# Pooling stage of a three-block network: window means as products of high and low parts, weight products by chunks, one root in place of an iteration

## The reference, cut to what matters

```
def rmsnorm(x, g):
    y = xf * lax.rsqrt(jnp.mean(xf * xf, axis=-1, keepdims=True) + NORM_EPS)
    return y * g

def pool_mixer(h, w_group, scale):          # h: the normed input, 4 groups of 256 channels
    csum = jnp.cumsum(hf, axis=1)
    for g, w in enumerate((2, 4, 8, 16)):   # mean over the last w tokens
        means.append((cg - prev) / cnt)
    mixed = pooled - hf
    y = jnp.einsum('blgc,gcd->blgd', mixed, w_group)
    return y * scale
...
h = h + rmsnorm(m, norm_mix_post[i])
```

## Time and profile before

| | us |
|---|---|
| median of 3 runs | 961.72 (961.63 to 963.1) |
| profiled execution | 959.84 |
| its span | 958.1 |
| products with `window_means` (L808) | 377.06 to 386.80 |

### The profile page before, as it was taken

The page is one execution under the profiler, slowest core; times in us unless marked ns, Lnnn a source line. Parts: engine busy times, 40 slices in busy tenths (PEclk is TensorE's granted clock), DMA queues, the critical chain, the costliest instruction groups (busy, mean ns, idle before and its releaser), DMA issues.

```text
span 958.1 us, 20030 instructions
## 1 busy us (share of the span) xinstructions
PE 920.1 (96%) x7354; PEld 890.3 (93%) x7354; DVE 685.8 (72%) x1168; ACT 513.3 (54%) x851; POOL 305.7 (32%) x215
## 2 busy tenths in 40 slices
PE   6999999999999998999999999999989999999996
PEld 6987798999999997899999999989989999999995
DVE  7766527999995225699999523879787878885666
ACT  5765555666665426666666544553355445454433
POOL 4117752000004543300001464331236333445643
PEclk9999999999999999999999999999999999999998
DMA  7541032444454541054455454344135455565431
GB/s 261 174 148 44 1 133 96 174 173 174 174 207 181 182 168 45 28 193 175 175 179 205 181 199 159 105 177 148 61 139 177 176 181 197 191 221 186 164 132 45
DMA packets 22147, 146.80 MB, mean 153 GB/s; under 512 B 2752, under 2 KB 5328, under 8 KB 6736
## 3 DMA queue, kind: packets, MB, share of 16 engines
q1 hardware_dynamic: 22096, 146.11, 42.9%
HBM read 143.94 MB, written 1.05 MB: 151 GB/s over the span
## 4 chain that ended last, share of the span: by engine, by line
PE 81%; DVE 12%; ACT 3%; issue 2%; POOL 1%; DMA 0%; POOLq 0%; SPq 0%; DVEq 0%; ACTq 0%
PE bank L439 22%; PE bank L440 22%; PE bank L441 22%; PE bank L693 2%; PE bank L679 2%; DVE u_low L1324 2%; DVE w_low L1315 2%; DVE h L1397 1%; PE bank L527 1%; ACT w_high L952 1%; DVE bank L1389 1%; DVE conv_out L1446 1%; PE bank L808 1%; PE bank L541 1%; PE bank L709 1%
## 5 line engine op out<-in xcount | busy, mean ns | idle before, releaser
L439 PE MATMUL bank<-u_high,w_high 128*128 128x256 f32 (+2 forms) x1400 | 401.1, 286 | 11.7 <-DVE u_low L1324 8.9
L440 PE MATMUL bank<-u_low,w_high 128*128 128x256 f32 (+2 forms) x1400 | 398.9, 285 | 0.0
L441 PE MATMUL bank<-u_high,w_low 128*128 128x256 f32 (+2 forms) x1400 | 397.6, 284 | 0.0
L1823 POOL TENSOR_TENSOR w_low<-raw,w_high 128x512 fp32r<-128x512 f32 (+1 forms) x73 | 199.8, 2738 | 543.7 <-ACT w_high L952 543.7
L1315 DVE TENSOR_TENSOR w_low<-raw,w_high 128x1024 fp32r<-128x1024 f32 (+5 forms) x119 | 189.9, 1596 | 125.5 <-ACT w_high L952 124.3
L439 PEld LDWEIGHTS bank<-u_high,w_high 128*128 128x128 f32 x1400 | 265.5, 190 | 14.3 <-DVE u_low L1324 8.4
L440 PEld LDWEIGHTS bank<-u_low,w_high 128*128 128x128 f32 x1400 | 265.1, 189 | 0.0
L441 PEld LDWEIGHTS bank<-u_high,w_low 128*128 128x128 f32 x1400 | 264.9, 189 | 0.0
L952 ACT ACTIVATE w_high<-raw 128x1024 fp32r<-128x1024 f32 (+5 forms) x119 | 195.2, 1640 | 72.0 <-PE bank L441 61.0
L439 PE MATMUL bank<-x_high,w_high 128*128 128x256 f32 (+1 forms) x608 | 173.9, 286 | 5.1 <-ACT x_high L1252 2.5
L441 PE MATMUL bank<-x_high,w_low 128*128 128x256 f32 (+1 forms) x608 | 173.2, 285 | 0.0
(11 more groups left out here) (213 smaller groups left out, 1057.7 us busy)
## 6 DMA issues: line engine op xcount, KB each, us to landing
raw<-w_up_dram SPq DMA_DIRECT2D x66, 1024.0 KB, 4.8
raw<-w_down_dram SPq DMA_DIRECT2D x24, 1408.0 KB, 6.0
raw<-w_gin_c_dram SPq DMA_DIRECT2D x4, 1536.0 KB, 6.5
raw<-w_wo_dram SPq DMA_DIRECT2D x4, 1024.0 KB, 5.1
raw<-w_wout_dram SPq DMA_DIRECT2D x4, 1024.0 KB, 4.9
raw<-w_pgate_dram SPq DMA_DIRECT2D x4, 1024.0 KB, 4.8
raw<-w_gin_v_dram SPq DMA_DIRECT2D x2, 1024.0 KB, 4.8
raw<-w_gin_g_dram SPq DMA_DIRECT2D x2, 1024.0 KB, 4.8
```

The source lines that it names most:

```text
L439: nc.tensor.matmul(out, hi, rhi, start=start, stop=False)
L440: nc.tensor.matmul(out, hi, rlo, start=False, stop=False)
L441: return nc.tensor.matmul(out, lo, rhi, start=False, stop=stop)
L1823: nc.gpsimd.tensor_tensor(wl[n % 2][:, at], raw[n % 2][:, at], wh[n % 2][:, at].bitcast(F32), ALU.subtract).then_inc(low_parts_g, pool_cou ...
```

## The change

1. **Means.** `pool_z` becomes two tiles, high (ScalarE) and low (VectorE, six new instructions of 512 columns). The means get a high part (three activations in `down0`) and a low part of the first 16 columns, the only ones whose values need one. Each chunk takes seven fp32r products in place of three fp32 ones, over the columns that a window reaches: 144, 144, 16, then 144, 144, then 16, 16. Chunks wait for the low parts.
2. **Weights' products by chunks.** Chunks 0 to 3 multiply for all three token tiles as they come, chunks 4 to 7 for the first tile; the sums follow, then the other two tiles of the second half.
3. **Root.** `a1` is normed by a square root on ScalarE and a reciprocal on VectorE in place of the iteration. VectorE makes the first half of `up1`'s low part ahead of that, the second half after the pooling.
4. **Results.** ScalarE only squares, into five buffers in place of two; VectorE writes the eight scaled copies.
5. The load of the means moves from behind the loads of `down0` to behind those of `up0`.

```diff
-BY_SQRT = ("c", "post0", "fpost0", "post1", "fpost1", "out")
+BY_SQRT = ("c", "post0", "fpost0", "a1", "post1", "fpost1", "out")
...
+REACH = [(0, P + 16), (P, P + 16), (2 * P, T1 - 2 * P)]
...
-                if name == "down0":
+                if name == "up0":
 
                     sp.wait_ge(*done("att out 7 low"))
                     sp.dma_start(wm[:, :, :], dram["window_means"]).then_inc(tables_in, 16)
...
+            for c in range(DC // 2):
+                pool_chunk(c, (0, 1, 2))
+            for c in range(DC // 2, DC):
+                pool_chunk(c, (0,))
+            norm_sums("a1", f"a1 acc {DC - 2}", squares(0, T1), True)
+            for t in (1, 2):
+                for c in range(DC // 2, DC):
+                    pool_chunk(c, (t,))
             pe.wait_ge(tables_in, 80)
+            pe.wait_ge(*done("window means low"))
             for c in range(DC):
                 half, g = c // 4, c // 2
 
-                pe.wait_ge(freed["a"], BLOCKS[first + half * len(TT) + len(TT) - 1]["freed"])
+                pe.wait_ge(*done(f"pool low {max(c, 2) if half == 0 else 5}"))
                 b = first + 2 * len(TT) + c
                 bank_free(b)
-                for t, (t0, nt_) in enumerate(TT):
-                    last = nc.tensor.matmul(bank[BLOCKS[b]["bank"]][:, t0:T1], pz[0:nt_, t, c * P:(c + 1) * P],
-                                            wm[0:nt_, g, WIN_AT[t]:WIN_AT[t] + T1 - t0],
-                                            start=t == 0, stop=t == len(TT) - 1)
+                out, cs = bank[BLOCKS[b]["bank"]], slice(c * P, (c + 1) * P)
+                for t, (t0, w) in enumerate(REACH):
+                    nt_ = TT[t][1]
+                    means = wmh[0:nt_, g, REACH_AT[t]:REACH_AT[t] + w]
+                    nc.tensor.matmul(out[:, t0:t0 + w], pzh[0:nt_, t, cs], means, start=t == 0, stop=False,
+                                     skip_group_check=True)
+                    last = nc.tensor.matmul(out[:, t0:t0 + w], pzl[0:nt_, t, cs], means, start=False,
+                                            stop=t == len(TT) - 1, skip_group_check=True)
+                    if t == 0:
+
+                        nc.tensor.matmul(out[:, 0:16], pzh[:, 0, cs], wml[:, g, :], start=False, stop=False,
+                                         skip_group_check=True)
                 last.then_inc(products, 1)
...
+                if l == 0:
+                    act.wait_ge(tables_in, 80)
+                    for t, (_, w) in enumerate(REACH):
+                        nc.scalar.activation(wmh[:, :, REACH_AT[t]:REACH_AT[t] + w], wm[:, :, WIN_AT[t]:WIN_AT[t] + w],
+                                             ACT.Copy).then_inc(*S.step("window means high"))
...
+            rms("a1", 3)
             act.wait_ge(*done("a1 1/rms"))
...
             for b in range(8):
-                post("post1", b, n, FIRST_BLOCK["pool"] + 2 * len(TT) + b, psg[:, b:b + 1], scale=pcol("pool_scale", b))
+                if b >= 5:
+                    act.wait_ge(*done(f"post1 acc {b - 5}"))
+                block_done(FIRST_BLOCK["pool"] + 2 * len(TT) + b)
+                nc.scalar.activation(pooled_sq[b % 5], bank[BLOCKS[FIRST_BLOCK["pool"] + 2 * len(TT) + b]["bank"]][:, 0:T1],
+                                     ACT.Square, scale=pcol("pool_scale", b)).then_inc(*S.step(f"post1 sq {b}"))
...
             norm("a1", tiles_of(T1))
+            dve.wait_ge(*S.now())
+            for half in range(2):
+                for t, (t0, nt_) in enumerate(TT):
+                    i = half * len(TT) + t
+                    x, cs = BLOCKS[FIRST_BLOCK["pool"] + i], slice(half * 512, (half + 1) * 512)
+                    dve.wait_ge(freed["a"], x["freed"])
+                    nc.vector.scalar_tensor_tensor(pzl[0:nt_, t, cs], bank[x["bank"]][0:nt_, :], nr[0:nt_, t:t + 1],
+                                                   pzh[0:nt_, t, cs].bitcast(F32), ALU.mult, ALU.subtract)\
+                        .then_inc(*S.step(f"pool low {i}"))
+            for b in range(DC):
+                x = BLOCKS[FIRST_BLOCK["pool"] + 2 * len(TT) + b]
+                dve.wait_ge(*done(f"post1 sq {b}"))
+                nc.vector.tensor_scalar(m[:, b, :], bank[x["bank"]][:, 0:T1], psg[:, b:b + 1], None, ALU.mult)\
+                    .then_inc(freed["a"], 1)
+            low_part(FIRST_UNIT["up1"], 1)
```

More of the change, by code:

```diff
@@ L524, in chunk_sums @@
                     x = sq[:, k % 2, c * P:(c + 1) * P]
+                    if name == "post1":
+                        x = pooled_sq[k % 5][:, c * P:min((c + 1) * P, T1)]
                     if name in SQUARES_IN_M:
@@ L779, in _ @@
             parts_ready(n)
-            for half in range(2):
-                for t, (t0, nt_) in enumerate(TT):
[L782 to L799, removed]
@@ new lines, in _, with pool_chunk @@
+            high_ready, low_ready = high_then_low("a1")
+            def pool_chunk(c, tiles):
+                half, g, k = c // 4, c // 2, c % 2
+                at = slice(c * 256, c * 256 + 256)
+                outs = []
+                for t in tiles:
+                    b, (t0, nt_) = first + half * len(TT) + t, TT[t]
+                    if c % 4 == 0:
+                        bank_free(b)
+                    outs.append((t, slice(t0, t0 + nt_),
+                                 bank[BLOCKS[b]["bank"]][0:nt_, (g % 2) * 256:(g % 2) * 256 + 256]))
+                high_ready(c)
+                for t, toks, out in outs:
+                    nc.tensor.matmul(out, uh[:, c, toks], wh[n % 2][:, at], start=k == 0, stop=False,
+                                     skip_group_check=True)
+                    nc.tensor.matmul(out, uh[:, c, toks], wl[n % 2][:, at], start=False, stop=False,
+                                     skip_group_check=True)
+                low_ready(c)
+                for t, toks, out in outs:
+                    last = nc.tensor.matmul(out, ul[:, c, toks], wh[n % 2][:, at], start=False, stop=k == 1,
+                                            skip_group_check=True)
+                    if c % 4 == 3:
+                        last.then_inc(products, 1)
@@ L989, in u_high, with post @@
                 square(name, c, h[:, c, t0:t0 + T], T, S.step(f"{name} sq {label}"), k, i)
[L991 removed]
+            def post(name, c, n, b, gain, k=None, i=None, stride=0):
                 T = SEQ if name == "fpost1" else T1
                 src = bank[BLOCKS[b]["bank"]][:, 0:T]
[L995 to L998, removed]
[L999 to L1005 removed]
+                block_done(b, i, stride)
+                square(name, c, src, T, S.step(f"{name} sq {c if k is None else k}"), k, i)
+                nc.scalar.activation(m[:, c, 0:T], src, ACT.Copy, scale=pcol(gain, c)).then_inc(freed["a"], 1)
             def ffn_up(l, T, conv, skip=0):
@@ L1332, in norm @@
                     dve.wait_ge(*done(f"{name} rms"))
-                    nc.vector.reciprocal(ny[:, 0:n], nt[:, 0:n]).then_inc(*S.step(f"{name} inverse"))
+                    if name == "a1":
+                        nc.vector.reciprocal(nr[:, 0:n], nt[:, 0:n]).then_inc(*S.step("a1 1/rms"))
+                    else:
+                        nc.vector.reciprocal(ny[:, 0:n], nt[:, 0:n]).then_inc(*S.step(f"{name} inverse"))
                     return
@@ L1375, in freed_wait, with low_part @@
                 dve.wait_ge(freed["v"], BLOCKS[b]["freed"] if i is None else 4 * i + BLOCKS[b]["freed"])
+            def low_part(n, part):
+                half, cols = first_half(n), vector_cols(n)
+                cs = slice(half, cols) if part else slice(0, half)
+                dve.wait_ge(high_parts, n + 1)
+                nc.vector.tensor_tensor(wl[n % 2][:, cs], raw[n % 2][:, cs], wh[n % 2][:, cs].bitcast(F32), ALU.subtract)\
+                    .then_inc(*((low_parts_v, 1) if part else S.step()))
             def add_post(name, nxt, gain, T, t0, unit):
@@ L1402, in add_post @@
                         u_low(nxt, c - 1, T, t0, gain)
-                low(unit)
+                if name == "fpost0":
+                    low_part(unit, 0)
+                else:
+                    low(unit)
             def ffn_up(l, T, conv, name, skip=0):
@@ L1603, in _ @@
             ffn_down_lows(0)
+            dve.wait_ge(*done("window means high"))
+            nc.vector.tensor_tensor(wml[:, :, :], wm[:, :, 0:16], wmh[:, :, 0:16].bitcast(F32), ALU.subtract)\
+                .then_inc(*S.step("window means low"))
             add_post("fpost0", "a1", "mix_pre1", T1, 0, FIRST_UNIT["down0"] + DC + 1)
             norm("a1", tiles_of(T1))
+            dve.wait_ge(*S.now())
[13 more added lines that the diff above has]
+            low_part(FIRST_UNIT["up1"], 1)
+            dve.wait_ge(freed["a"], x["freed"])
             add_post("post1", "f1", "ffn_pre1", SEQ + HISTORY, META - HISTORY, FIRST_UNIT["pool"] + 2)
```

24 lines of the change are left out of this document (12 added, 12 removed).

## The result

The changed kernel takes **965.94 us** (median of 20 runs, 962.6 to 968.38); the kernel before, beside it, 962.38 (20 runs, 959.61 to 964.8). The ratio is 1.0033, with a 95% interval of 1.0021 to 1.0045: slower by a third of a per cent. The prediction was 965.6, range 960.0 to 967.8, with 62% on slower.

What follows compares the result with a forecast made beforehand. TensorE was taken to bound the stage: 0.0 (start) - 1.4 (chunk price) + 3.1 (slow chunks) + 2.2 (slow sums) = +3.9 us. From the profiled 959.84 that gives 963.7, against the median 965.6; range 960.0 to 967.8.

Steps and rivals of the forecast that it cites:

- What bounds the kernel: TensorE, on 81% of the chain; the stage up to `add_post("post1")` at 391.16 decides the worth, neighbouring stages unchanged.
- Part 1, the start: Start of the products with the means, before at 377.06: 0.0 us, from -1.0 to +2.2.
- The sum: All terms over the stage together: 0.0 - 1.4 + 3.1 + 2.2 = +3.9 us.
- the prediction's worst: Start of the means: all 24 products after the sums run at 1.2 GHz, bound +2.2 us.
- Part 2, the price of a chunk: Products with the means at full clock: 1.04 us a chunk against 1.22 before, 8.3 in all, -1.4.
- Part 3, the clock: Means and their sums: clock falls after about five chunks, +3.1 us for the last three, +2.2 for the sums.
- the signs named for being right: Clock 0.50 between 380 and 390, chunks about 2.1 us behind chunks about 1.1, sums over 4 us.
- Covered parts: GpSimd, ScalarE, VectorE, `down0` and the means' load stay hidden: 0 us, at worst +1 if the load lands late.
- The clock holds: TensorE has no idle row between chunks of means, so no fall: -2.4 us, 959.3, down to 957.2; 20%.
- Narrow fp32r at the price of fp32: A 144-column product with the means costs 2 x 0.13 us, a chunk 1.64, +3.4, clock holds: 965.1; 20%.
- The late fall: Only the last chunk of means and half the sums are slow: +0.2 us, 961.9, no change; 15%.

Runs made afterwards that it cites:

- e6: The kernel before with only norm `a1` changed, to a square root and a reciprocal in place of the iteration: 961.96 us, 0.9995 of before.
- e9: The changed kernel with the first half's third-tile products moved ahead of chunks 4 to 7, six products in each wait: 963.83 us, 1.0021 of before.
- e2: The changed kernel plus 18 unread products of 272 columns in the waits behind chunks 4 to 7: 963.55 us, 1.0020 of before.
- e7: The changed kernel with the third tile's weights zero-filled to 128 rows, columns still narrow: 961.91 us, 1.0000 of before.
- e1: The changed kernel with the products with the means back in plain fp32, all else as changed: 961.08 us, 0.9994 of before.
- e4: The changed kernel with four of seven products over 272 columns and the third tile's weights zero-filled to 128 rows: 958.38 us, 0.9962 of before.
- e10: e4 with the first half's third-tile products moved ahead of chunks 4 to 7, six products in each wait: 958.08 us, 0.9957 of before.
- e8: The changed kernel with the first two tiles' products over all 272 columns, the third tile still at 16 rows: 962.14 us, 0.9997 of before.
- e3: The changed kernel plus two unread products of 512 columns behind each of the eight chunks of means: 963.95 us, 1.0018 of before.

## Why the prediction was right, point by point

- **What bounds the kernel.** Right. The stage went from 31.03 to 36.17 us, +5.1 in the traces, and the stages around it issue what they issued. The first `add_post` came at 361.36 against 360.13, with a fall of the clock at 161.84 that the trace of before does not have. Six of the twelve traces have that fall, e6 with the `down0` of before among them, and their first `add_post` comes at 361.22 to 361.98; in the six without it, it comes at 359.65 to 360.61. So this is scatter between executions and no part of the change. `down0`'s first high part comes 1.33 us later than before (283.86 against 282.53), as much as the load ahead of that of the means does (263.47 against 262.14), so the earlier load delayed nothing.
- **Part 1, the start: mis-sized.** The sum had 0.0, and the stage shows +1.26 (7.16 against 5.90). Both halves of the term were right in kind. The gain at full clock was -1.0 and is -0.7 (5.19 in e9). For the clock I took half of the 24 products under 1.2 GHz; it was all of them, and from 373.46 on the end of the sums ahead of them too. The case that ran is the prediction's worst, all 24 slow: that is -1.0 + 2.2 = +1.2 (its upper bound of +2.2 left the gain out). e9 and e2 show the cause named there: without the threes of products the fall is gone.
- **Part 2, the price of a chunk: right.** 1.04 predicted, 1.02 to 1.03 measured. Its two terms are apart in e7: seven loads at 0.112 are 0.79 (0.78 predicted), and the row changes 0.24 (0.26). The Trainium skill ("TensorE: Matmul & The Clock Gate", Back-to-back issue gap) gives about 81 ns for a product of 128 columns with its load. By that figure I estimate e7's chunk at 7 x 0.081 = 0.57 us. The trace, with 0.79, does not agree for these four-byte weights.
- **Part 3, the clock: right in kind and place.** It fell in the fourth chunk (I said after about five), with TensorE busy all through. A slow chunk cost 1.80, not 2.08, and the sums 3.87, not over 4: two of the signs named for being right came out smaller. e7's slow chunk is 1.50, 0.214 a load and not 0.224, and the change of rows hardly grows, from 0.24 to 0.30, where I had doubled it. The means cost +1.92 against a forecast of -1.4 + 3.1 = +1.7. The sums cost +1.62, against +2.2. The slower sums and the longer fall also cost the rows behind 0.30, which had 0 in the sum. Together 1.26 + 1.92 + 1.62 + 0.30 = +5.1 in the traces, where the sum had +3.9, and +3.6 between the medians: the trace of before is one of its kernel's better executions (e6, with the same products, has a stage of 32.60, 3.6 under after's). That 965.6 lies 0.3 from the median is in part luck: the start was missed by 1.3, the sums by 0.6 the other way, and what a trace of a median execution of before would show is not known.
- **Covered parts: right.** e1 has them all at 0.9994. ScalarE's three activations took 1.39 us (1.5 predicted), and VectorE's new low parts 3.37/5 = 0.67 each (0.68 predicted). GpSimd's sums waited for ScalarE in after; only at e4's and e10's pace do they bind, for some 0.2 us (0.39 less 0.18).
- **Rivals.** *The clock holds*: refuted. The row from 380.29 to 383.70 has TensorE's products busy for 3.41 of 3.41 us (its loads for 3.03) and 1.00 of the clock, and the next has 0.50; in e7 products and loads are both busy for 3.15 of 3.15 us, and the clock falls all the same. The rule named there from the Trainium skill ("TensorE: Matmul & The Clock Gate", What's actually happening), that the array keeps 2.4 GHz while busy, does not agree with these rows where busy is read off them. *Narrow fp32r at the price of fp32*: refuted. In e7 the seven products of a chunk, four of them of 144 columns, start 0.112 apart on average; at 0.26 for each of the four a chunk would be over 1.37. It would have given 965.1, close to the truth for a wrong reason, and only the row tells. *The late fall*: the single executions of after range from 962.6 to 968.4 us; the fastest seven, 962.6 to 963.8, have a mean granted clock of 0.981 to 0.984, the other thirteen 0.976 to 0.980. So those seven spend less time at 1.2 GHz. Whether they spare it in the stage, as this rival has it, or outside, stays open, since no run among the seven has a trace.

## What to carry to other kernels

Before replacing wide products by more and narrower ones, ask what the array streams between two weight loads: here the clock fell in chunks of seven loads with 624 columns and held in those with 1136 (0.9997 of before against 1.0033), though 512 of the columns multiply zeros. Where an engine waits in small steps, try to spread the work it has over all the waits and not to use it up in the first ones. In e9 and e10 that took a fall of the clock away; that it makes the whole faster is not clear of noise. Look at the next stretch too, since with the first fall gone the next came sooner (e2, e9). And move the norm or the scale off the path only when something waits for it: in e6 nothing did, and it was worth nothing.

## What the runs showed of the hardware

- The granted clock fell with TensorE's matmul rows busy without a gap (after, 383.70) and with matmul and load rows both so (e7, 384.06), and held through the same loads when each chunk streamed 272 columns in four of its seven products (e8), or had two more products of 512 (e3).
- fp32r products of 144 and of 16 columns follow one another at the pace of one-column products, 0.112 us each at 2.4 GHz (e7; the earlier trace rows), and at 0.214 at 1.2 GHz. So the weight load is what bounds them.
- Going from weights of 128 rows to weights of 16 and back costs 0.24 us a chunk at 2.4 GHz, 0.30 at 1.2 GHz (after against e7), and with wide columns 1.12 less 0.83 = 0.29 (e8 against e4).
- Filling 112 rows with zeros to avoid that cost TensorE nothing: in e7 the third tile's two products start 0.07 apart (381.06 and 381.13), with 16 rows 0.13 apart (380.54 and 380.67 in after).
- A stretch at 1.2 GHz lasted 17 us in after while the work stayed in narrow products, sums and rows; before, the fall behind the sums was over after 3.4 us.
